# Order of the paged steps in a hybrid decoder step: queries' products beside the weighted sums, next latents turned in the third and fourth slot

## The reference

```python
def step(carry, phys):
    c_blk = cache_ckv[layer, phys]          # 128 latent rows of 256
    kp_blk = cache_kpe[layer, phys]         # 128 rotary key rows of 32
    kn_blk, v_blk = _decompress(c_blk, w_ukv, g_kn)   # keys get an RMS norm per head
    return _merge(carry, _attn_partial(qn, qp, kn_blk, kp_blk, v_blk, None)), None
```

## Time and profile before

| what | value |
| --- | --- |
| median of 3 runs | 1353.2 us (1346.31 to 1353.28) |
| profiled execution, its own time | 1355.08 us |
| its span, first to last instruction | 1353.0 us |
| mean granted TensorE clock | 0.977 of full speed |
| PE busy | 1295.4 us, 96% |
| DVE busy | 716.1 us, 53% |
| ACT busy | 459.0 us, 34% |
| norms of the pages, PE L502 | 502.6 us, 1024 passes |
| latent transposes, PE L455 | 82.0 us, 512 passes |

### The profile page before, as it was taken

One profiled execution on the slowest core, in us unless ns is written; L12 is line 12 of the kernel. 1 busy time (PEld: TensorE's weight loads), 2 busy tenths in 40 slices (PEclk: granted clock), 3 DMA queues, 4 the chain that ended last, 5 costly groups with the idle time before them and its releaser, 6 DMA issues. The chain is left out here.

```text
span 1353.0 us, 25936 instructions
## 1 busy us (share of the span) xinstructions
PE 1295.4 (96%) x9479; PEld 741.5 (55%) x9479; DVE 716.1 (53%) x1781; ACT 459.0 (34%) x1108; POOL 152.1 (11%) x182
## 2 busy tenths in 40 slices
PE   6999999889999999999989998999999999989898
PEld 3545677656665666664544445666544444445343
DVE  3000448644566666564647776877666666530321
ACT  3001354233343433332434433433444444310220
POOL 0000326400010102033302240000000000000000
PEclk9999999989999999998989999999999999998899
DMA  6422121111111111310231113321233212101000
GB/s 208 158 70 60 33 63 32 53 37 38 37 38 37 37 36 38 72 37 18 67 106 40 45 48 100 107 95 36 86 116 116 85 55 64 39 0 35 16 16 35
DMA packets 82994, 81.48 MB, mean 60 GB/s; under 512 B 18946, under 2 KB 76611, under 8 KB 82868
## 3 DMA queue, kind: packets, MB, share of 16 engines
q1 hardware_dynamic: 80452, 73.87, 18.2%
q10 hardware_dynamic: 2416, 5.96, 1.3%
HBM read 75.72 MB, written 4.07 MB: 59 GB/s over the span
## 5 line engine op out<-in xcount | busy, mean ns | idle before, releaser
L502 PE MATMUL PS<-wk,c_T 128*128 128x512 f32 x1024 | 502.6, 614 | 0.0
L632 DVE TENSOR_REDUCE ssq<-sq__69 128x8 f32<-128x512 f32 x256 | 175.5, 685 | 223.0 <-ACT sq__69 L557 220.2
L502 PEld LDWEIGHTS PS<-wk,c_T 128*128 128x128 f32 x1024 | 177.1, 193 | 166.2 <-issue 150.3
L557 ACT ACTIVATE sq__69<-PS 128x512 f32<-128x512 f32 x256 | 152.7, 596 | 306.9 <-PE PS L502 306.9
L1491 PE MATMUL PS<-xnT,w_ring 128*128 128x276 f32 x416 | 101.0, 400 | 0.0
L1329 PE MATMUL PS<-w_ring,xnT 128*128 128x424 f32 x256 | 96.6, 535 | 0.9 <-DVE xnT L985 0.9
L455 PE MATMUL PS<-cst,c_ring 128*128 128x128 f32 x512 | 82.0, 284 | 10.2 <-DVE c_T L623 6.2
L1491 PEld LDWEIGHTS PS<-xnT,w_ring 128*128 128x128 f32 x416 | 77.8, 190 | 20.6 <-issue 4.1
L455 PEld LDWEIGHTS PS<-cst,c_ring 128*128 128x128 f32 x512 | 59.7, 146 | 52.9 <-issue 23.9
L1329 PEld LDWEIGHTS PS<-w_ring,xnT 128*128 128x128 f32 x256 | 48.8, 194 | 45.5 <-issue 45.5
L2697 PE MATMUL PS<-w_g,nT 128*128 128x512 f32 x128 | 56.0, 594 | 0.0
(11 more groups left out here) (533 smaller groups left out, 1839.2 us busy)
## 6 DMA issues: line engine op xcount, KB each, us to landing
c_ring<-in_cache_ckv SPq DMA_DIRECT2D x256, 128.0 KB, 2.8
w_ring<-in_w_in SPq DMA_DIRECT2D x4, 1696.0 KB, 12.3
w_ring<-in_w_in SPq DMA_DIRECT2D x9, 512.0 KB, 5.0
r_ring<-in_cache_kpe SPq DMA_DIRECT2D x256, 16.0 KB, 1.8
w_o<-in_w_out SPq DMA_DIRECT2D x8, 512.0 KB, 4.1
w_g<-in_w_ple_gate SPq DMA_DIRECT2D x8, 512.0 KB, 3.6
xn<-in_x_prompt SPq DMA_DIRECT2D x4, 512.0 KB, 10.9
w_ring<-in_w_in SPq DMA_DIRECT2D x2, 1024.0 KB, 6.1
```

The costliest lines, as they stand in the source:

```text
L502: mm = pe.matmul(PS[:, NORM[v % 2], :], c_T[:, u % 2, k, t * P:(t + 1) * P], wk[:, k], start=(k == 0), stop=(k == 1))
L557: nc.scalar.activation(sq_[:, v % 2, :], PS[:, NORM[v % 2], :], ACT.Square).then_inc(no_sb, 1)
L632: dve.tensor_reduce(ssq[:, u % 2, t * H:(t + 1) * H], sq_[:, v % 2, :].rearrange("p (h c) -> p h c", h=H), AX.X, ALU.add).then_inc(red_sb, 1)
```

## The change

Seven edits, all in the order of work and in where things are kept:

1. On PE, `turn_r(u)` moves to slot 0, `dots(u)` to slot 1 right ahead of `values(u - 2)`, and the two halves of the next step's latents to slots 2 and 3. Semaphores follow: `turn_c(u, 0)` waits for the copied products of step u - 1, `turn_r(u)` for the copied second half of its own step.
2. ACT copies the first half (slot 2), DVE the second (slot 3). DVE copies the products in slot 1, ahead of the merge; ACT the turned rotary rows in slot 0.
3. The copied products have two buffers, the score is written over them, and `sc` goes. The copy waits for the exponentials of step u - 2.
4. The rotary ring has three steps in place of four, and SP waits for the transpose of step u - 3 before it asks for step u.
5. In the preparation SP asks for the pages of two steps of the generator, in place of four.
6. The start's semaphore is split: ACT and PE wait for the constants, DVE for the norm row.
7. `wukv2` is asked for behind the last sequence products, and PE waits for the weights ahead of the first products of the latent stage.

```diff
@@ pages_sp
+                if u >= R_RING:
+                    sp.wait_ge(tn_ps, u - R_RING + 1)
...
@@ pages_pe
             def turn_c(u, k):
                 if k == 0:
                     pe.wait_ge(c_in[u % RING], 16 * GT * (u // RING + 1))
-                    if u == 1:
-                        pe.wait_ge(k1_sb, 1)
-                    if u >= 2:
-                        pe.wait_ge(rp_sb, u - 1)
+                    if u >= 1:
+                        pe.wait_ge(rp_sb, u)
...
             def turn_r(u):
-                pe.wait_ge(r_in[u % RING], 16 * GT * (u // RING + 1))
-                if u + 1 < NSTEP:
-                    pe.wait_ge(k1_sb, u + 2)
-                else:
-                    pe.wait_ge(rp_sb, u)
+                pe.wait_ge(r_in[u % R_RING], 16 * GT * (u // R_RING + 1))
+                pe.wait_ge(k1_sb, u + 1)
...
                 if t == 0:
-                    if ahead:
-                        turn_c(u + 1, 0)
+                    turn_r(u)
                     if u >= 2:
                         turn_weights(u - 2)
                 if t == 1:
-                    if ahead:
-                        turn_c(u + 1, 1)
+                    dots(u)
                     if u >= 2:
                         values(u - 2)
                 if t == 2:
-                    turn_r(u)
+                    if ahead:
+                        turn_c(u + 1, 0)
                     if u >= 1:
                         turn_scale(u - 1)
-                if t == 3:
-                    dots(u)
+                if t == 3 and ahead:
+                    turn_c(u + 1, 1)
                 norms(u, t)
@@ pages_act (turned_c now copies the first half)
                 if t == 0:
+                    turned_r(u)
                     if u >= 2:
                         turned_weights(u - 2)
                     if u >= 1:
                         roots(u - 1)
-                    square(u, t)
-                if t == 1:
-                    if ahead:
-                        turned_c(u + 1)
-                    square(u, t)
-                if t == 2:
-                    turned_r(u)
-                    square(u, t)
-                if t == 3:
-                    if u >= 1:
-                        weights(u - 1)
-                    square(u, t)
+                if t == 2 and ahead:
+                    turned_c(u + 1)
+                if t == 3 and u >= 1:
+                    weights(u - 1)
+                square(u, t)
@@ pages_dve (turned_c now copies the second half)
             def dotted(u):
                 dve.wait_ge(rp_ps, u + 1)
-                dve.tensor_copy(dots_s[:].rearrange("p x c -> p (x c)"), PS[:, TURN, P:3 * P]).then_inc(rp_sb, 1)
+                if u >= 2:
+                    dve.wait_ge(eq_sb, u - 1)
+                dve.tensor_copy(dots_s[:, u % 2].rearrange("p x c -> p (x c)"), PS[:, TURN, P:3 * P]).then_inc(rp_sb, 1)
...
-                if t == 0:
-                    if ahead:
-                        turned_c(u + 1)
-                    if u >= 1:
-                        scales(u - 1)
-                if t == 1 and u >= 2:
-                    merge(u - 2)
+                if t == 0 and u >= 1:
+                    scales(u - 1)
+                if t == 1:
+                    dotted(u)
+                    if u >= 2:
+                        merge(u - 2)
                 if t == 2 and u >= 1:
                     score(u - 1)
-                if t == 3:
-                    dotted(u)
+                if t == 3 and ahead:
+                    turned_c(u + 1)
                 reduce(u, t)
@@
-        on_sp = Stream(pages_sp(), lambda slot: min(NSTEP, max(RING, (slot - 2) // GT + RING - 1)))
+        on_sp = Stream(pages_sp(), lambda slot: 2 if slot <= PREP_SLOTS else min(NSTEP, max(RING, (slot - 2) // GT + RING - 1)))
@@ start
-                act.dma_start(norm_row[:], io["rows"][:, 0:D].to_broadcast([P, D])).then_inc(first_in, 16)
-                act.wait_ge(first_in, 32)
+                act.dma_start(norm_row[:], io["rows"][:, 0:D].to_broadcast([P, D])).then_inc(norm_in, 16)
+                act.wait_ge(first_in, 16)
...
-                dve.wait_ge(first_in, 32)
+                dve.wait_ge(norm_in, 16)
@@ seqs_sp, behind on_sp.go(SEQ_SLOTS - 5)
+            sp.wait_ge(gh_ps, PAIRS)
+            sp.dma_start(wukv2[:], io["w_ukv"].rearrange("(k p) c -> p k c", p=P)).then_inc(w_lat2, 16)
@@ lat_sp
-            sp.dma_start(wukv2[:], io["w_ukv"].rearrange("(k p) c -> p k c", p=P)).then_inc(w_lat2, 16)
@@ lat_pe
             on_pe.go(3)
-            pe.wait_ge(w_lat2, 32)
...
                 pe.wait_ge(ct_dve, i + 1)
+                if i == 0:
+                    pe.wait_ge(w_lat2, 32)
```

More of the change, by code:

```diff
@@ L132 @@
 RING = 4
+R_RING = 3
 QH = H * TS
@@ L245, in build @@
         ssq = place("ssq", [P, 2, GT * H])
-        dots_s = place("dots_s", [P, 2, P])
+        dots_s = place("dots_s", [P, 2, 2, P])
         rep = place("rep", [P, GT * QH])
-        sc = place("sc", [P, P])
         ew_q = place("ew_q", [P, P])
@@ L254, in build @@
         r_T = place("r_T", [P, P])
-        r_ring = place("r_ring", [P, RING, GT * ROPE])
+        r_ring = place("r_ring", [P, R_RING, GT * ROPE])
         w_ring_at = t1_at + 4 * (NT * D + KD * TEXT)
@@ L372, in w_due @@
             return 16 * sum(len(c) for x, c in enumerate(chunks[:n + 1]) if x % 2 == n % 2)
-        first_in, aux_in, w_lat, table_in, pages_in = kept_sems("first_in", "aux_in", "w_lat", "table_in", "pages_in")
+        first_in, norm_in, aux_in, w_lat, table_in, pages_in = kept_sems("first_in", "norm_in", "aux_in", "w_lat", "table_in", "pages_in")
         x_in = kept_sems(*(f"x_in_{i}" for i in range(NT + 1)))
@@ L409, in build @@
         c_in = kept_sems("c_in0", "c_in1", "c_in2", "c_in3")
-        r_in = kept_sems("r_in0", "r_in1", "r_in2", "r_in3")
+        r_in = kept_sems("r_in0", "r_in1", "r_in2")
         slots = [(u, t) for u in range(NSTEP) for t in range(GT)]
@@ L434, in pages_sp @@
                     latent_pages(u, page)
+                if u >= R_RING:
+                    sp.wait_ge(tn_ps, u - R_RING + 1)
                 for x in range(GT):
                     p4 = slice(32 * x, 32 * x + 32)
-                    sp.dma_start(r_ring[p4, u % RING, :],
+                    sp.dma_start(r_ring[p4, u % R_RING, :],
                                  io["cache_kpe"][bass.ds(page[x], 1)].rearrange("o (p t) c -> (o p) (t c)", t=GT)
-                                 ).then_inc(r_in[u % RING], 16)
+                                 ).then_inc(r_in[u % R_RING], 16)
                 yield
@@ L458, in turn_r @@
             def turn_r(u):
-                pe.wait_ge(r_in[u % RING], 16 * GT * (u // RING + 1))
-                if u + 1 < NSTEP:
-                    pe.wait_ge(k1_sb, u + 2)
-                else:
-                    pe.wait_ge(rp_sb, u)
-                pe.transpose(PS[:, TURN, 0:P], r_ring[:, u % RING, :], ident).then_inc(tn_ps, 1)
+                pe.wait_ge(r_in[u % R_RING], 16 * GT * (u // R_RING + 1))
+                pe.wait_ge(k1_sb, u + 1)
+                pe.transpose(PS[:, TURN, 0:P], r_ring[:, u % R_RING, :], ident).then_inc(tn_ps, 1)
             def dots(u):
@@ L544, in turned_c @@
             def turned_c(u):
-                act.wait_ge(k1_ps, u + 1)
-                nc.scalar.copy(c_T[:, u % 2, 1, :], PS[:, TURN, :]).then_inc(k1_sb, 1)
+                act.wait_ge(k0_ps, u + 1)
+                nc.scalar.copy(c_T[:, u % 2, 0, :], PS[:, TURN, :]).then_inc(k0_sb, 1)
             def turned_r(u):
@@ L571, in weights @@
                 nc.scalar.activation(ms[:, 3:4], ms[:, 2:3], ACT.Exp).then_inc(al_sb, 1)
-                nc.scalar.activation(ew_q[:], sc[:], ACT.Exp, bias=ms[:, 1:2]).then_inc(eq_sb, 1)
+                nc.scalar.activation(ew_q[:], dots_s[:, u % 2, 1, :], ACT.Exp, bias=ms[:, 1:2]).then_inc(eq_sb, 1)
             def turned_weights(u):
@@ L578, in turned_weights @@
                 nc.scalar.copy(ew[:], PS[:, MISC, at_t]).then_inc(ew_sb, 1)
+            turned_c(0)
             yield
-            turned_c(0)
             yield
@@ L621, in turned_c @@
             def turned_c(u):
-                dve.wait_ge(k0_ps, u + 1)
-                dve.tensor_copy(c_T[:, u % 2, 0, :], PS[:, TURN, :]).then_inc(k0_sb, 1)
+                dve.wait_ge(k1_ps, u + 1)
+                dve.tensor_copy(c_T[:, u % 2, 1, :], PS[:, TURN, :]).then_inc(k1_sb, 1)
             def dotted(u):
                 dve.wait_ge(rp_ps, u + 1)
-                dve.tensor_copy(dots_s[:].rearrange("p x c -> p (x c)"), PS[:, TURN, P:3 * P]).then_inc(rp_sb, 1)
+                if u >= 2:
+                    dve.wait_ge(eq_sb, u - 1)
+                dve.tensor_copy(dots_s[:, u % 2].rearrange("p x c -> p (x c)"), PS[:, TURN, P:3 * P]).then_inc(rp_sb, 1)
             def reduce(u, t):
@@ L646, in score @@
             def score(u):
-                nm = nmax[:, u // STEPS:u // STEPS + 1]
```

(11 more changed lines are left out.)

## The result

The changed kernel ran at 1332.1 us (median of 4 runs, 1327.7 to 1332.9) beside 1353.2 for the one before (1346.3 to 1353.4): ratio 0.9847, 95% interval 0.9821 to 0.9873, 21 us less. The forecast was 1324, the range 1311 to 1340. The profiled execution, 1327.7 us with a span of 1325.6, is the fastest of the four, so what follows adds up to the 27.4 us between the two spans and not to 21. A stand is time in which PE has nothing to run; a stretch of lower clock is one in which the granted clock reads about half (0.50 to 0.51 where a window holds nothing else).

A forecast was written before the change was run, and what follows sets the result against it. TensorE's (PE's) instruction stream, busy 96% of the span, was taken as the bound. Terms of 5.3 + 0.9 + 9.6 + 2.5 + 6.6 + 2 + 1.8 = 28.7 us off 1353.2 gave 1324 us, range 1311 to 1340.

The forecast's parts named there:

- The narrow blocks: Slot 1: rotary products and weighted sums merge into one narrow block, saving 0.36 us a step, bounds 0 and 0.42.
- Rival (b): Slot 1: the two narrow blocks don't merge, 15.8 us of the sum go, 1340 us; chance 0.07.
- (c): Narrow block in slot 1: the sums' weight loads stay exposed, 62 x 0.16 = 10 us, 1334 us; chance 0.07.
- The new wait in slot 0: Rotary transpose waits for DVE's second-half copy, giving back 0.12 us a tail step; 0.25 stays, -5.3 us over 21 steps.
- rival (a): DVE takes over as limit; mixed stages and tail lose their gain to the slot 0 wait, 1338 us; chance 0.13.
- Stands in the mixed stages: PE's stands on DVE's latent copies shrink, -2.5 of 6.2 us, bounds +6 and -6; Gram masks leave about 1.8.
- the mark for being wrong: Slot 0: the prediction is wrong if PE's waits for the second-half copy exceed 10 us.
- The weights: Latent stage start: earlier weight request removes a 3.9 us stand and lower clock behind it, -6.6 us, bounds -3.9 and -8.
- The preparation: Before the barrier: fewer SP page requests let the chunk stage start sooner despite a new 2.3 us stand; -2 us.
- The start: First wait split: ACT goes ahead without the norm row, DVE starts at 7.95 instead of 9.76; -1.8 us.
- The mixed and attention steps: Shorter slots: 0.1 us in each of 8 attention steps, -0.9; 31 other mixed steps, latent ones counted half, -9.6.
- The slower case (d): Slot 0: second-half copy late in most of 39 mixed steps, +59 us, 1383; decides from 0.74 a step; chance 0.05.

The follow-up runs named there:

- copy_first: Changed kernel with DVE's copy of the second latent half put ahead of the reduce of slot 2, which moves into slot 3; 1320.4 us, ratio 0.9757.
- weights_back: Changed kernel with only the wukv2 request back behind wuq2 and its wait back at the head of the latent stage; 1335.4 us, ratio 0.9889.
- pages_back: Changed kernel with SP's page requests of the preparation put back (four steps of rotary pages, a fourth of latents); 1329.3 us, ratio 0.9849.
- blocks_apart: Changed kernel with the weighted sums ahead of the rotary product in slot 1, a full-width pair between the narrow blocks; 1346.4 us, ratio 0.9959.
- split_all: Changed kernel with early step-0 rotary pages; ACT copies second halves (steps 33-41: DVE, ahead of the reduce) and products, step 32's included; 1316.2 us, ratio 0.9733.
- early_rope: Changed kernel with the rotary pages of step 0 requested with its latent pages, some 15 us earlier; 1330.8 us, ratio 0.9841.
- one_wait: Changed kernel with only the first wait joined again, constants and norm row together; 1332.9 us, ratio 0.9867.

## Why the prediction was right, and where it was off

**The narrow blocks: right, also in size.** 0.36 us of a tail step were forecast before any wait. The tail of copy_first, which has the changed kernel's PE order and no stand, gives 9.85 - 9.50 = 0.35, and putting a full-width pair between the blocks costs 0.34 there. Rival (b), that they don't merge, is out. So is (c): the sums' eight loads (944.89) lie inside the products' matmuls. The Trainium skill (TensorE: Matmul & The Clock Gate, Part 3, what overlaps and what doesn't) lets a weight load overlap a running matmul only if it sits in another row group, though the mechanism given in the same Part also names a background weight buffer as a target; here both use all 128 rows and differ in columns, and they overlap.

**The new wait in slot 0: the term that was mis-sized.** I had DVE reach the reduce at slot 2's start + 3.13, the copy end at + 4.42 and PE go on at + 4.51, 0.12 behind its own + 4.39. Measured: reduce + 3.22, copy + 3.82 to + 4.50, PE + 4.65; PE alone would be there at + 4.41. The stand is 0.24. The chain in the earlier trace rows was DVE's; in the new step DVE is idle 0.23 for ACT's square, which starts 0.26 after the norm has streamed, and the copy's signal reached PE's matmul after 0.15, not 0.09. The reduce was counted from the wrong engine's row. So 0.10 a step stays in place of 0.25, and 2 us of the 5.3; for two thirds of the tail's gain rival (a) was right. copy_first shows the rest: take the wait away and it is all there.

**Stands in the mixed stages: place right, price short.** The Gram masks give 1.89 us at 356.9 by the slot's length (1.7 in the waits view), forecast 1.8; the products' copy at the end of the latents gives 3.6, where I had carried over the old 2.5. All waits on DVE's copies come to 5.2 + 4.7 = 9.9 us against 6.2 for the latent halves and 1.4 for the products before: +2.3 in place of -2.5. Rival (a) had this direction. The chunk and sequence steps kept their 0.33, but in the latent stage it was partly true: steps 27 and 31 gained 0.06 and 0.07, and copy_first, where DVE's copy comes sooner, brings both to 0.33. With the 21 stands of 0.24 the wait for the second half comes to 5.2 + 5.0 = 10.2 us, just over the 10 that I had named as the mark for being wrong; the mark was set without counting the tail's stands, which the sum had.

**The weights: right in kind, 1 to 3 us too high.** 6.6 forecast, 5.0 between the traces and 3.3 to 5.7 between the runs. The stand went, and its stretch of lower clock with it; in weights_back that stretch costs about 0.05 x 35 = 1.7 us by the windows view, where I had 2.7 from the longer one of the kernel before.

**The preparation: wrong.** -2 forecast, nothing measured. The new stand is there (2.9 us, forecast 2.3), and the barrier does follow the later of SP and DVE. But I took its moving from SP's time to DVE's for a gain of two: with the stand, followed by the lower level (PEclk 0.57 from 255 to 263 in the windows view), DVE's last copy ends at 273.35, and the stage begins 1.65 behind it, as it begins 1.62 behind SP's last request in pages_back. The stand had made DVE as late as SP had been, and from then on SP's earlier end buys 0.2 us.

```profile
255.00:263.00 8.00, 5.08 (x27) 2.49 (x24) 1.72 (x5) 0.86 (x2) 0.02 (x1) 0.57 0.06 16
```

**The start: right**, 1.8 us, kept to the end.

**The mixed and attention steps: right in the first two stages, less behind them.** In the chunk stage a step with no stand in either kernel is 0.33 us shorter (for instance 16.66 to 16.33, 18.15 to 17.81). Of the 31, I had 0.36 for 22 and half of that for nine. The nine latent steps can't be told one by one, as waits moved within them. Attention gave 0.05 a step, not 0.1. The direction was right, but the 0.30 of the earlier trace rows was not the stand of each step, as I had it: in six of eight PE stood under 0.1 us, and there the wait for the probability grew to 0.36 and took 0.28 of the 0.33 that the order saves.

**Sum.** Forecast 28.7, measured 21.1: 3.3 too much in the tail, some 4.8 for the stands on copies, 2 in the preparation, 0.4 in attention, 1 to 3 for the weights, 11 to 13 together. So 4 to 6 us came that no term has, and their source stays open. In the two traces the clock gives some (25 us lost to it instead of 31, of which the forecast had priced 2.7; steps 19 and 20, with less of it than before, gained 2.0 and 1.5 us where their undisturbed neighbours gained 0.33). But at the same granted clock of 0.980 the spans are 1349.5 to 1352.0 in seven executions of the kernel before and 1330.6 and 1330.8 in two of the changed one, 19 to 21 us apart, so the clock can't be much of the medians' 21. PE's waits for a latent page (1.1 us before, none after) and for DVE's nat (2.1 and 1.1) are 2 us shorter. No run here isolates either. In the number this was luck: without it the time would have been 1336 to 1338, where rival (a) had its 1338, and 1332 itself is nearer to (c)'s 1334 than to 1324. What tells the forecast from them is copy_first's tail step of 9.50 us and blocks_apart's of 10.10, not the time, and not the 9.76 alone. The slower case (d) did not come: only five steps had a stand on that copy by the waits view, the longest 1.7 us, where it needed 0.74 and more in most of 39.

**Best version.** copy_first is the changed kernel with one edit and has 0.9757; split_all, with four, has 0.9733, and their intervals overlap widely. Both are faster than both kernels.

## What to carry to other kernels

Put matmuls of one narrow array shape side by side: a full-width pair between two such blocks costs a third of a microsecond here where full-width work lies around them, and 0.14 us where other narrow pieces lie ahead. When an edit makes an engine's copy the last thing before PE, follow the chain that feeds it back through the other engines (norm, square, reduce, copy) and not only that engine's own row of before; then put the copy first in its slot. A stand that vanishes from the waits view may be in the slot lengths, and one that moves from consumer to consumer belongs to the producer in front of all of them.

## What the runs showed that was not expected

The stretches of lower clock fell at other places in nearly every kernel, and moved results by 1 to 3 us: early_rope was 2.4 us ahead at 290 us and 0.9 behind at 688. A change worth less than that is read from the trace (one_wait, pages_back), not from the runs. Between executions of one kernel it is more: of the experiments' executions of the kernel before, four with a granted clock of 0.983 had spans of 1344.0 to 1345.2 us, seven with 0.977 had 1350.7 to 1353.6.

Many stretches came behind stands, the barriers' among them, but not all. PE of the changed kernel, ten microseconds without a wait and the stretch behind them:

```profile
204.90:214.90 10.00, 10.00 (x51) 6.38 (x50) 7.94 (x17) 3.71 (x7) 5.14 (x5) 1.00 0.27 78
```

```profile
214.90:218.30 3.40, 3.40 (x9) 2.54 (x8) 3.40 (x6) 0.00 (x0) 3.40 (x3) 0.51 0.24 83
```

What PE had just done there were sixteen matmuls in 32x32 pieces (from 210.99 on); ahead of the one at 600.6 us, also with no wait over 0.2 us in the ten before, it was mostly matmuls in 64x64 pieces of four columns. Why a particular stand or such a block was followed by a stretch and another was not stays open.
